# A three-layer transformer kernel on one core: another order of loads and head preparation ahead of the first attention, and other places for the over-capacity branch at the end

## The reference

```
qa_l, qs_l, kva_l, kr_l, ks_l, vs_l = split_cols(h_lat @ w_in, EVEN_Q_SIZES + EVEN_KV_SIZES)
q_mla = mla_queries(qa_l, q_norm, w_qb, cos32, sin32)          # rms_norm(q_a) @ w_qb, part of it rotated
k_mla_l, v_mla_l = mla_keys_values(kva_l, kr_l, kv_norm, w_kvb, cos32, sin32)
```

## Time and profile before

| | |
|---|---|
| three runs | 1757.74, 1761.36, 1764.48 us; median 1761.36 |
| the profiled execution | 1759.84 us, of which its span 1758.0 |
| TensorE busy | 1676.2 us, 95% of the span, 10590 matmuls |
| VectorE, ScalarE busy | 1032.7 us (59%), 835.0 us (47%) |
| TensorE's granted clock | 0.987 of full speed, mean |
| DMA | 287.80 MB, 164 GB/s |
| chain that ended last | TensorE 80%, VectorE 11%, ScalarE 5%, issue 3%, DMA 1% |

### The profile page before, as it was taken

The page is one execution under the profiler, slowest core; times in us unless marked ns, Lnnn a source line. Parts: engine busy times, 40 slices in busy tenths (PEclk is TensorE's granted clock), DMA queues, the critical chain, the costliest instruction groups (busy, mean ns, idle before and its releaser), DMA issues.

```text
span 1758.0 us, 25543 instructions
## 1 busy us (share of the span) xinstructions
PE 1676.2 (95%) x10590; PEld 1359.1 (77%) x10590; DVE 1032.7 (59%) x1512; ACT 835.0 (47%) x1202; POOL 0.9 (0%) x5
## 2 busy tenths in 40 slices
PE   8989999999999999999898999999998999999996
PEld 5736566777877787898588999899887867777775
DVE  3436655534334444535756666657776658888885
ACT  3435543543223322523736454555454437766764
POOL 0000000000000000000000000000000000000000
PEclk9999999999999999999999999999999999999998
DMA  9212623153334514233023454344232419999983
GB/s 392 101 54 97 216 96 145 72 192 134 142 136 152 193 67 174 85 118 116 5 73 135 156 205 166 132 152 160 100 116 73 144 61 375 344 336 344 355 320 116
DMA packets 42823, 287.80 MB, mean 164 GB/s; under 512 B 4800, under 2 KB 5952, under 8 KB 11600
## 3 DMA queue, kind: packets, MB, share of 16 engines
q1 hardware_dynamic: 42528, 285.99, 44.6%
q10 hardware_dynamic: 144, 0.06, 0.0%
q0 software_dynamic: 32, 0.07, 0.0%
HBM read 285.05 MB, written 1.05 MB: 163 GB/s over the span
## 4 chain that ended last, share of the span: by engine, by line
PE 80%; DVE 11%; ACT 5%; issue 3%; DMA 1%; DVEq 0%; ACTq 0%; SPq 0%
PE ps L512 16%; PE ps L514 15%; PE ps L513 15%; PE ps L2793 5%; DVE WL L497 4%; PE ps L2763 2%; PE ps L2767 2%; PE ps L2764 2%; PE ps L557 2%; PE ps L1527 1%; PE ps L1429 1%; PE ps L1498 1%; PE ps L537 1%; PE ps L675 1%; PE ps L2669 1%
## 5 line engine op out<-in xcount | busy, mean ns | idle before, releaser
L512 PE MATMUL ps<-HH,WH 128*128 128x512 f32 (+2 forms) x1488 | 495.4, 333 | 22.2 <-DVE WL L497 12.4
L497 DVE TENSOR_TENSOR WL<-ring,WH 128x2048 fp32r<-128x2048 f32 (+2 forms) x192 | 413.4, 2160 | 147.6 <-ACT WH L487 147.3
L514 PE MATMUL ps<-HH,WL 128*128 128x512 f32 (+2 forms) x1488 | 483.6, 325 | 0.0
L513 PE MATMUL ps<-HL,WH 128*128 128x512 f32 (+2 forms) x1488 | 483.1, 325 | 0.0
L487 ACT ACTIVATE WH<-ring 128x2048 fp32r<-128x2048 f32 (+2 forms) x192 | 347.0, 1809 | 194.5 <-PE ps L514 75.7
L512 PEld LDWEIGHTS ps<-HH,WH 128*128 128x128 f32 x1488 | 284.1, 191 | 69.2 <-issue 28.5
L514 PEld LDWEIGHTS ps<-HH,WL 128*128 128x128 f32 x1488 | 284.1, 191 | 21.7
L513 PEld LDWEIGHTS ps<-HL,WH 128*128 128x128 f32 x1488 | 284.8, 191 | 20.0 <-issue 0.2
L512 PE MATMUL ps<-parts,WH 128*128 128x512 f32 (+1 forms) x352 | 119.7, 340 | 0.0
L513 PE MATMUL ps<-parts,WH 128*128 128x512 f32 (+1 forms) x352 | 118.4, 336 | 0.0
L514 PE MATMUL ps<-parts,WL 128*128 128x512 f32 (+1 forms) x352 | 118.2, 336 | 0.0
(11 more groups left out here) (371 smaller groups left out, 2242.2 us busy)
## 6 DMA issues: line engine op xcount, KB each, us to landing
ring<-wts SPq DMA_DIRECT2D x196, 1024.0 KB, 5.0
arena<-wts SPq DMA_DIRECT2D x46, 1024.0 KB, 6.8
ring<-wts SPq DMA_DIRECT2D x32, 704.0 KB, 4.0
ring<-wts SPq DMA_DIRECT2D x4, 672.0 KB, 13.6
X<-xin SPq DMA_DIRECT2D x4, 512.0 KB, 16.3
cst<-csts SPq DMA_DIRECT2D x1, 1395.0 KB, 20.0
ring<-wts SPq DMA_DIRECT2D x3, 384.0 KB, 4.1
out<-arena SPq DMA_DIRECT2D x2, 512.0 KB, 2.9
```

Source lines behind the costliest of these rows:

```text
L497: e.tensor_tensor(lo, raw(i), hi.bitcast(F32), ALU.subtract).then_inc(*up("low", i))
L512: e.matmul(o, w[0][:, cols], x[0], start=k == 0, stop=False)
L513: e.matmul(o, w[0][:, cols], x[1], start=False, stop=False)
L514: return e.matmul(o, w[1][:, cols], x[0], start=False, stop=k == nk - 1)
```

## The change

At the start, both query chunks are loaded ahead of the four `mod` chunks. TensorE does a `mod` chunk ahead of each of the first two tiles and one on either side of the third, takes the sums for both norms together, and prepares heads 0 and 1 ahead of the last tile; in `pe_heads` the rotations of the two queries come ahead of the value tiles. ScalarE makes the second chunk's high part ahead of the roots, VectorE its low part ahead of the norms, and ScalarE's copies for the two heads move with them.

At the end, the last chunk of each group's down projection is done half by half, with a signal for each; each engine's branch moves ahead of its part of the last group's scatter (TensorE: between the last down projection and the scatter; ScalarE and VectorE: after their last weight split); ScalarE takes a root of a constant ahead of the squares; TensorE does three matmuls of no use between the sums and the spread; the output goes out in three pieces (4, 3 and 1 of 8 blocks). The over-capacity code's own waits are changed to suit.

```diff
@@ chunk_plan
-    for i in range(2):
-        p += [(("abq", i), 2048), (("mod", 0, 8 + i), 2048)]
-    p += [(("mod", 0, i), 2048) for i in (10, 11)]
+    p += [(("abq", i), 2048) for i in range(2)]
+    p += [(("mod", 0, i), 2048) for i in range(8, 12)]
@@ pe_inputs
             c = [index["abq", i] for i in range(2)]
+            pe_mod(e, 0, 8)
             pe_tiles(e, c[0], ((0, 128, "kept.qs", 0),), False)
             e.wait_ge(*VEC)
             e.wait_ge(*CST)
             pe_rms(e, "kept.qa", [SQ[:, m, :] for m in range(2)], "o256")
+            pe_rms(e, "kept.kv", [HT[:, 1, :]], "o128")
+            pe_mod(e, 0, 9)
             pe_tiles(e, c[0], ((128, 128, "kept.qs", 1),))
-            pe_mod(e, 0, 8)
-            pe_rms(e, "kept.kv", [HT[:, 1, :]], "o128")
...
-            pe_tiles(e, c[1], ((0, 128, "kept.qs", 2),), False)
             e.wait_ge(*at("kept.ks"))
             pe_rope(e, ("kept.ks",), KS, 128, "r128")
             e.wait_ge(*at("kept.kr"))
             pe_rope(e, ("kept.kr",), KR, 96, "r96")
+            pe_mod(e, 0, 10)
+            pe_tiles(e, c[1], ((0, 128, "kept.qs", 2),), False)
+            pe_mod(e, 0, 11)
+            pe_mod_end(e)
+            e.wait_ge(*at("unit", "kept.kv", 0))
+            for h in range(2):
+                pe_prepare(e, h)
             pe_tiles(e, c[1], ((128, 128, "kept.qs", 3),))
-            for i in range(9, 12):
-                pe_mod(e, 0, i)
-            pe_mod_end(e)
@@ act_inputs
+            c = [index["abq", i] for i in range(2)]
+            act_high(e, c[1], 1)
             e.wait_ge(*VEC)
             e.wait_ge(*CST)
             act_rms_root(e, "kept.qa", RS[:, :])
-            c = [index["abq", i] for i in range(2)]
+            act_rms_root(e, "kept.kv", HT[:, 2, :])
             act_keep(e, QS[:, 0, :], 128, ("kept.qs", 0), at("tile", "kept.qs", 0))
-            act_high(e, c[1], 1)
...
-            act_mod(e, 0, 8)
-            act_rms_root(e, "kept.kv", HT[:, 2, :])
...
             act_keep(e, QS[:, 2, :], 128, ("kept.qs", 2), at("tile", "kept.qs", 2))
+            for i in range(8, 12):
+                act_mod(e, 0, i)
+            for h in range(2):
+                act_prepare(e, h)
             act_keep(e, QS[:, 3, :], 128, ("kept.qs", 3), at("used", c[1]))
-            for i in range(9, 12):
-                act_mod(e, 0, i)
@@ dve_inputs
             dve_low(e, c[0], 1)
+            dve_low(e, c[1], 1)
...
             dve_rms(e, "kept.qa", 2, RS[:, :], lambda m: QA[:, m, :], "qnorm", lambda m: QN[:, m, :])
-            dve_low(e, c[1], 1)
-            dve_mod(e, 0, 8)
@@ pe_heads
-            e.wait_ge(*at("unit", "kept.kv", 0))
             for h in range(2):
-                pe_prepare(e, h)
+                pe_query_rope(e, h)
...
-            for h in range(2):
-                pe_query_rope(e, h)
@@ act_heads
-            for h in range(2):
-                act_prepare(e, h)
@@ pe_stat, pe_stat_spread
-                    pe_warm(e, warm, 5, x)
+                    pe_warm(e, warm, 3 if tag == "fin" else 5, x)
...
-            b = bank(e, "stat_spread", tag)
+            b = banks.of["stat_spread", tag] if tag == "fin" else bank(e, "stat_spread", tag)
@@ pe_expert_out
+                for n in range(2):
+                    for k in range(2, 4):
...
+                            t = e.matmul(ps[:, bs[n], :], HTE[p][:, z, hs], w[q][:, s], start=False, stop=k == 3 and p == 1)
+                    t.then_inc(*(up("used", c) if n else up("tile", "ey", y)))
@@ pe_experts
             pe_expert_out(e, NE - 1)
+            with over_capacity(e, "pe"):
+                pe_over(e)
             pe_scatter(e, 3)
@@ act_expert_out
             act_high(e, index["ed", x, 1])
+            if x == NE - 1:
+                with over_capacity(e, "act"):
+                    act_over(e)
             if x % 4 == 3:
                 y = x // 4
-                e.wait_ge(*at("used", index["ed", x, 1]))
                 if y:
                     e.wait_ge(*at("scatter", y - 1, 7))
                 for n in range(2):
+                    e.wait_ge(*(at("used", index["ed", x, 1]) if n else at("tile", "ey", y)))
@@ dve_expert_out
             dve_low(e, index["ed", x, 1])
+            if x == NE - 1:
+                with over_capacity(e, "dve"):
+                    dve_over(e)
@@ tensor_program
             pe_experts(e)
-            with over_capacity(e, "pe"):
-                pe_over(e)
             bank(e, "stat", "fin")
+            b = bank(e, "stat_spread", "fin")
             for j in range(8):
-                pe_stat(e, "fin", j, SQF)
+                pe_stat(e, "fin", j, SQF, b, split_parts(index["ed", NE - 1, 1])[0])
@@ scalar_program
-            with over_capacity(e, "act"):
-                act_over(e)
+            e.activation(small[:, 126:127], EPS6, ACT.Sqrt)
@@ sync_program
-            for h in range(2):
-                e.wait_ge(*at("normed", "fin", 4 * h + 3))
...
-            e.wait_ge(s_out, 32)
+            for a, z in ((0, 4), (4, 7), (7, 8)):
+                e.wait_ge(*at("normed", "fin", z - 1))
+                e.dma_start(out.rearrange("p (j t) -> p j t", j=8)[:, a:z, :], OUT[:, a:z, 16:NT]).then_inc(s_out, 16)
+            e.wait_ge(s_out, 48)
```

More of the change, by code:

```diff
@@ L2788, in pe_expert_out @@
                     hs = slice(128 * k, 128 * k + 128)
-                    first, last = x % 4 == k == 0, x % 4 == k == 3
+                    if x % 4 == 3 and i:
+                        break
                     for p, q in ((0, 0), (0, 1), (1, 0)):
@@ L2792, in pe_expert_out @@
                             s = slice(1024 * (k - 2 * i) + 512 * n, 1024 * (k - 2 * i) + 512 * n + 512)
-                            t = e.matmul(ps[:, bs[n], :], HTE[p][:, z, hs], w[q][:, s], start=first and p == q == 0,
-                                         stop=last and p == 1)
-                t.then_inc(*up("used", c))
+                            t = e.matmul(ps[:, bs[n], :], HTE[p][:, z, hs], w[q][:, s], start=x % 4 == k == p == q == 0,
+                                         stop=False)
+                if x % 4 < 3 or i == 0:
+                    t.then_inc(*up("used", c))
+                    continue
+                for n in range(2):
+                    for k in range(2, 4):
+                        hs = slice(128 * k, 128 * k + 128)
+                        s = slice(1024 * (k - 2) + 512 * n, 1024 * (k - 2) + 512 * n + 512)
+                        for p, q in ((0, 0), (0, 1), (1, 0)):
+                            t = e.matmul(ps[:, bs[n], :], HTE[p][:, z, hs], w[q][:, s], start=False, stop=k == 3 and p == 1)
+                    t.then_inc(*(up("used", c) if n else up("tile", "ey", y)))
             if x % 4 == 3:
@@ L2944, in pe_over @@
         def pe_over(e):
-            e.wait_ge(*at("added", 3, 7))
+            over_banks.order = [b for b in range(8) if b not in (banks.of["ey", 3, 0], banks.of["ey", 3, 1])]
+            e.wait_ge(*at("low", index["ed", NE - 1, 1]))
             e.wait_ge(*at("over_added.comb"))
@@ L2976, in act_over @@
         def act_over(e):
-            e.wait_ge(*at("added", 3, 7))
+            e.wait_ge(*at("used", index["ed", NE - 1, 1]))
             for x in range(NE):
@@ L2986, in dve_over @@
         def dve_over(e):
-            e.wait_ge(*at("added", 3, 7))
-            e.wait_ge(*at("y_high", 3, 1))
+            e.wait_ge(*at("used", index["ed", NE - 1, 1]))
             for c in range(3):
@@ L3106, in vector_program @@
             dve_experts(e)
-            with over_capacity(e, "dve"):
-                dve_over(e)
             dve_stat_norm(e, "fin", "nfin", OUT)
@@ L3137, in sync_program @@
                 sp_over(e)
-            for h in range(2):
-                e.wait_ge(*at("normed", "fin", 4 * h + 3))
-                e.dma_start(out.rearrange("p (j t) -> p j t", j=8)[:, 4 * h:4 * h + 4, :],
-                            OUT[:, 4 * h:4 * h + 4, 16:NT]).then_inc(s_out, 16)
-            e.wait_ge(s_out, 32)
+            for a, z in ((0, 4), (4, 7), (7, 8)):
+                e.wait_ge(*at("normed", "fin", z - 1))
+                e.dma_start(out.rearrange("p (j t) -> p j t", j=8)[:, a:z, :], OUT[:, a:z, 16:NT]).then_inc(s_out, 16)
+            e.wait_ge(s_out, 48)
         def pool_program(e):
```

## The result

The changed kernel takes 1745.87 us (median; 1745.36 to 1746.48) against 1761.54 for the kernel before: ratio 0.9912, 95% interval 0.9893 to 0.9932.

The account below looks back on a forecast made before the run. TensorE, busy for nearly the whole span, was taken to bound the kernel. Start 9.2 us and end 1.6 − 1.2 + 0.9 + 0.6 + 0.5 = 2.4 made 11.6 us: 1749.8 us forecast, range 1745.5 to 1755.

Parts of the forecast that it names:

- The start: From the first projection to the first scores: 1.31 + 3.59 + 1.7 + 2.59 = 9.2 us gained, scores at 98.8.
- 1.7 us of slow clock: First head's four matmuls behind the late load: 3.62 us at half clock, 1.96 for the next head; 1.7 gained.
- the vanished gap: TensorE's 3.59 us wait ahead of the first head, for the late head weights' load, goes.
- The branch: TensorE's jump over the over-capacity code, moved ahead of the last scatter: costs 2.86 us, scatter 1.39 later.
- half clock for the scatter: Last scatter: the new gap ahead of it brings the lower clock, costing 1.2 us.
- the sums' gain: TensorE's 64 sums at the end follow the squares, ending at 1746.6 instead of 1748.2: 1.6 us gained.
- rival (a): End: TensorE's branch is cheap in its new place or the clock stays up; 1745.8 to 1748.6, chance 0.25.
- The groups: Three earlier expert groups: copies of the expert sums start earlier; 0.5 us gained, bounds 0 and 1.5.
- The output: Final store in three pieces, the last of 128 KB: 0.6 us gained, 0.8 at best, nothing at worst.
- (b): Start: VectorE's norms and rotations or the head weights' landing hold up the heads; 1753 to 1757, chance 0.17.
- (c): Start: the head weights' load has a long tail, 20.0 us as the constants had; 1765, chance 0.03.
- rival (d): End: the branch only changes which gap it fills, the 1.6 is zero or negative; 1751 to 1754.5, chance 0.1.

Follow-up runs that it names:

- end-only kernel: Kernel before with all edits except those to the load plan, inputs and head preparation; 1755.44 us, ratio 0.9962.
- heads in place: Changed kernel with the preparation of heads 0 and 1 back behind the last query tile; span 1746.7 us.
- bare-branch kernel: Changed kernel with TensorE waiting for its own last expert matmul, so that the array is drained, ahead of its branch; span 1747.1 us.
- start-only kernel: Kernel before with only the edits to the load plan, inputs and head preparation; 1752.31 us, ratio 0.995.
- rotations after values: Changed kernel with the rotations of the first two queries back behind the four value tiles; span 1749.3 us.

## Why the prediction was right, and where its sizes were off

**The start: right.** 9.2 us forecast, 8.8 measured, scores at 99.22 for 98.8. Of its margins, the low half was made at 64.2 (forecast 64.1), the heads began at 83.57 (83.0). Two attributions do not stand as told. The 1.7 us of slow clock is in the profiled execution of before, but the end-only kernel had the same late load at full clock, so it is not in every execution. And the text ascribes the vanished gap to the heads' move and the earlier slots together; the run with the heads in place shows that the slots alone did it.

**The branch: the step that failed.** "I take 2.86, since the code jumped over is the same: scatter from 1742.46, 1.39 later than before." The idle time was taken for the branch's length, and moved with it. The stop for the branch is 4.3 to 4.8 us long, longer than taken, and yet costs nothing in the new place (at most 0.35 us in the other executions), because the sequencer meets it with matmuls still queued and the last of the wait lies beside VectorE's low part. The scatter came 0.9 us earlier relative to the last expert matmul (0.60 for 1.46), not 1.4 later: a mis-size of 2.3 us. The half clock for the scatter, 1.2 us, hung on that gap and was not there either; the bare-branch kernel shows that it would have been. The rest of the sums' gain (adds and squares straight away, the last 8 sums behind them) came much as told, 4.5 us from the scatter's start to the sums' end for 4.1, and so did the spread at full clock, 0.8 for 0.9. The three warming matmuls have no part in that: without them the spread was as fast. In time this was rival (a), 1745.8 to 1748.6, though for another reason: the branch is not cheap, it is hidden. That the median lies inside the stated range, 0.4 us above its lower end, is owed to that rival's price and not to the sum, which was 3.9 us off. There is luck in that too: the branch was taken as too short and as bare, two mistakes that work against each other.

**The groups: under-sized by the waits, open in whole time.** 0.5 us forecast. By the experts' waits it is 1.0 to 2.0 (6.8 to between 4.8 and 5.8), of which the split gives 0.3 to 1.3; the 1.1 between the marks is no measure, as the start-only kernel shows.

**The output: over-sized.** 0.6 forecast, 0.07 measured. The time of the last store was taken from that of a small load; here it stands behind the rest of the output in full DMA engines. The text had named that as its lower bound ("nothing at worst, as all three share the queues").

Sum: start 8.8 for 9.2, middle 1.1 for 0.5, end 4.5 for 1.9 (2.4 less the groups' 0.5). Rivals (b) and (c) did not come: in the changed kernel TensorE never waited for the head weights or for the norms. In rival (d) the working and the range do not fit: with the 1.6 us gone, or 1.3 below zero, the sum gives 1751.4 to 1752.7, not up to 1754.5. The median of the kernel before stands 1.7 above its profiled execution and that of the changed one 0.6 below, which makes 15.7 out of 14.4 less the change in what lies around the span (1.84 and 2.88).

## What to carry to other kernels

On TensorE, a check that jumps over a long stretch of code stopped the sequencer, not the array: place it right behind the issue of long work that no longer waits for anything, and ahead of a wait that is on another engine anyway. An idle time read from a trace is what is left of a delay after its cover, so it can't be moved with the instruction; count from the last event that the issuing side had to wait for. When a load is late, look first at what frees its slot: an earlier use of the slot's old contents was enough, where moving the consumer gave nothing.

## What the runs showed of the hardware that was not expected

- TensorE's stop for the branch is 4.3 to 4.8 us wherever it can be counted. In the three stops taken apart it is 1.7 to 1.9 us to the fetch of 16 KB of instructions, 1.0 to 1.3 us of fetch, 1.5 to 1.6 us to the next matmul. Matmuls already issued go on meanwhile. ScalarE's and VectorE's stops lie in idle time and can't be read.
- The clock behind an idle time is not set by its length alone: it stayed at the 2.4 GHz level (granted clock 1.00) behind 2.59 us (before), 2.43 and 2.99 us (end only), and was at the 1.2 GHz level behind 2.43 (rotations after values), 2.86 and 3.59 (before) and 4.51 us (drained branch). Ahead of the first scores 2.43 us of idle time was followed by either level. The matmuls right behind such a fall took 1.7 us longer (before, first head), 1.6 (drained, scatter) and 3.2 (rotations after values, two groups of four), so a short wait on TensorE can cost more than its length. Executions of one kernel differ with the clock: of the start-only kernel's four, two had a mean granted clock of 0.987 to 0.988 and took 1750.4 us, two had 0.986 and took 1754.2 and 1755.5.
- A store of 128 KB right behind one of 384 KB landed 2.8 us after its issue, as that one did: the DMA engines moved 356 to 358 GB/s without a pause for all of the output.
